# Attention over a memory in halves: queries, keys, probabilities and values as high and low parts, loaded head by head

## What is computed

```python
mem_n = rmsnorm(mem, mem_norm)                                   # 256 x 1024
mk, mv = jnp.split(mem_n @ mem_w_kv[i], 2, axis=-1)              # 4 heads of 256 columns each
...
def memory_attention(zq, mem_k, mem_v):                          # zq: part of h @ w_in, 512 x 1024
    s = jnp.einsum('bthd,bmhd->bhtm', q, mem_k) * (XA_DIM ** -0.5)
    p = jax.nn.softmax(s, axis=-1)
    o = jnp.einsum('bhtm,bmhd->bthd', p, mem_v)
```

## Time and profile before

| | us |
|---|---|
| median of three runs | 2362.25 (2361.05 to 2362.57) |
| profiled execution | 2362.44 |
| its span | 2360.7 |
| TensorE busy | 2340.6 (99%) |
| VectorE busy | 1197.9 (51%) |
| ScalarE busy | 743.0 (31%) |
| GpSimd busy | 263.3 (11%) |
| clock granted to TensorE | 0.998 |

### The profile page before, as it was taken

The page is one execution under the profiler, slowest core; times in us unless marked ns, Lnnn a source line. Parts: engine busy times, 40 slices in busy tenths (PEclk is TensorE's granted clock), DMA queues, the critical chain, the costliest instruction groups (busy, mean ns, idle before and its releaser), DMA issues.

```text
span 2360.7 us, 29488 instructions
## 1 busy us (share of the span) xinstructions
PE 2340.6 (99%) x10944; PEld 1943.6 (82%) x10944; DVE 1197.9 (51%) x1411; ACT 743.0 (31%) x1005; POOL 263.3 (11%) x235
## 2 busy tenths in 40 slices
PE   9999999999999999999999999999999999999998
PEld 9988888877888888888878888887788888888887
DVE  6654443446888654444445444344337644444422
ACT  4432222234444322222223223123333322322322
POOL 3400001111333420000110000120001212000000
PEclk9999999999999999999999999999999999999999
DMA  7733333332222333333333333333233233333322
GB/s 233 215 98 96 94 94 98 98 107 63 72 71 78 100 91 97 98 98 98 97 90 91 96 98 98 98 98 98 70 94 88 83 96 107 98 98 94 93 95 92
DMA packets 400691, 234.32 MB, mean 99 GB/s; under 512 B 7692, under 2 KB 386672, under 8 KB 400624
## 3 DMA queue, kind: packets, MB, share of 16 engines
q1 hardware_dynamic: 397328, 223.37, 32.1%
q0 software_dynamic: 3280, 10.02, 1.2%
q10 hardware_dynamic: 16, 0.00, 0.0%
HBM read 227.07 MB, written 6.29 MB: 99 GB/s over the span
## 4 chain that ended last, share of the span: by engine, by line
PE 95%; DVE 2%; ACT 1%; issue 1%; DMA 0%; POOL 0%; ACTq 0%; DVEq 0%; SPq 0%; POOLq 0%
PE acc L1012 26%; PE acc L1014 26%; PE acc L1013 26%; PE acc L766 1%; PE acc L768 1%; PE acc L767 1%; PE mix L398 1%; PE mix L385 1%; PE acc L249 1%; PE acc L251 1%; PE acc L250 1%; PE mix L250 1%; PE mix L249 1%; PE mix L251 1%; PE mix L833 1%
## 5 line engine op out<-in xcount | busy, mean ns | idle before, releaser
L1174 DVE TENSOR_TENSOR w_lo<-raw,w_hi 128x1024 fp32r<-128x1024 f32 (+1 forms) x422 | 548.3, 1302 | 658.4 <-ACT w_hi L1444 647.8
L1012 PE MATMUL acc<-h_hi,w_hi 128*128 128x512 f32 x1920 | 759.2, 395 | 7.5 <-DVE h_lo L1236 5.3
L1014 PE MATMUL acc<-h_hi,w_lo 128*128 128x512 f32 x1920 | 748.4, 390 | 0.0
L1013 PE MATMUL acc<-h_lo,w_hi 128*128 128x512 f32 x1920 | 747.9, 390 | 0.0
L1444 ACT ACTIVATE w_hi<-raw 128x1024 fp32r<-128x1024 f32 (+1 forms) x422 | 436.5, 1038 | 354.3 <-DMA raw<-in_ffn_w_out_dram 222.0
L1012 PEld LDWEIGHTS acc<-h_hi,w_hi 128*128 128x128 f32 x1920 | 361.3, 188 | 85.2 <-DVE h_lo L1236 6.6
L1013 PEld LDWEIGHTS acc<-h_lo,w_hi 128*128 128x128 f32 x1920 | 361.2, 188 | 77.0 <-issue 3.7
L1014 PEld LDWEIGHTS acc<-h_hi,w_lo 128*128 128x128 f32 x1920 | 360.9, 188 | 75.6
L1012 PE MATMUL acc<-act_hi,w_hi 128*128 128x512 f32 (+1 forms) x976 | 368.7, 378 | 2.6 <-DVE act_lo L1185 1.7
L1014 PE MATMUL acc<-act_hi,w_lo 128*128 128x512 f32 (+1 forms) x976 | 366.2, 375 | 0.0
L1013 PE MATMUL acc<-act_lo,w_hi 128*128 128x512 f32 (+1 forms) x976 | 366.1, 375 | 0.0
(11 more groups left out here) (214 smaller groups left out, 1779.0 us busy)
## 6 DMA issues: line engine op xcount, KB each, us to landing
raw<-in_ffn_w_in_dram SPq DMA_DIRECT2D x176, 512.0 KB, 3.7
raw<-in_ffn_w_out_dram SPq DMA_DIRECT2D x70, 512.0 KB, 4.0
raw<-in_hgrn_w_in_dram SPq DMA_DIRECT2D x40, 512.0 KB, 3.7
raw<-in_gmlp_w_in_dram SPq DMA_DIRECT2D x40, 512.0 KB, 3.6
raw<-in_mem_w_kv_dram SPq DMA_DIRECT2D x32, 512.0 KB, 4.2
raw<-in_gmlp_w_out_dram SPq DMA_DIRECT2D x24, 512.0 KB, 4.0
raw<-in_ffn_w_out_dram SPq DMA_DIRECT2D x24, 384.0 KB, 3.4
raw<-in_hgrn_w_out_dram SPq DMA_DIRECT2D x16, 512.0 KB, 4.0
```

What stands on the lines that cost most here:

```text
L1012: pe.matmul(bank, w_hi[:, j, i, :], hi, start=(start and i == 0), stop=False)
L1013: pe.matmul(bank, w_hi[:, j, i, :], lo, start=False, stop=False)
L1014: m = pe.matmul(bank, w_lo[:, j, i, :], hi, start=False, stop=(stop and i == last))
L1174: dve.tensor_tensor(w_lo[:, j, 0:nkb], raw[:, j, 0:nkb], f32(w_hi[:, j, 0:nkb]), ALU.subtract).then_inc(w_lo_ready, 1)
```

## The change

Keys and values are split when they are taken: for a K block VectorE's take stays, ScalarE writes the rounded half (`k_top`), VectorE the rest (`k_rest`); for a V block ScalarE takes two banks as before and then writes their rounded halves, VectorE subtracts in the next quad (`v_rest`), and after the last quad. A store carries both halves, 256 KB for 128 before, from buffers of its own (`k_parts`, `v_parts`), and waits for the rest half; the rounded half of a lane waits until the lane's last store has landed. The second copies of a V pair wait for the first ones.

In the attention q becomes a take (VectorE), a rounding copy (ScalarE) and a rest (VectorE); the turned probabilities a rounding copy (as the copy before) and a rest. The products are three fp32r matmuls each. The K and V of heads 0 and 1 are loaded when the phase begins, those of heads 2 and 3 into the same places when head 0's and 1's products are done (`load_later`, on GpSimd's queue): 8 loads of 256 KB, then 8 more.

```diff
-    k_scratch = nc.dram_tensor("k_scratch", (16, P, MEM), F32).ap()
-    v_scratch = nc.dram_tensor("v_scratch", (16, P, MEM), F32).ap()
+    k_scratch = nc.dram_tensor("k_scratch", (16, 2, P, MEM), F32).ap()
+    v_scratch = nc.dram_tensor("v_scratch", (16, 2, P, MEM), F32).ap()
...
+        k_parts = act_hi[:, 8:12, :].rearrange("p j (z m) -> p j z m", z=2)
+        v_parts = act_hi[:, 12:16, :].rearrange("p j (z m) -> p j z m", z=2)
...
+                slots = halves_at(kv_at, 8).rearrange("p (n b) (k m) -> p n b k m", n=2, k=2)
+                self.k = [[slots[:, n, part, :, :] for part in range(2)] for n in range(2)]
+                self.v = [[slots[:, n, 2 + part, :, :] for part in range(2)] for n in range(2)]
...
+                self.q_hi, self.q_lo = halves_at(q_hi_at, 4), halves_at(q_lo_at, 4)
+                self.p = work[:, p_at:p_at + 2, :].rearrange("p b (k m) -> p (b k) m", k=2)
+                self.pT_hi, self.pT_lo = halves_at(pT_hi_at, 2), halves_at(pT_lo_at, 2)
...
+                return 16 * 2 * (2 * self.layer + h // 2 + 1)
+            def load_half(self, pool, into, scratch, h, done):
+                b = DB * self.layer + 2 * h
+                for z in range(2):
+                    pool.dma_start(into[:, 2 * z:2 * z + 2, :],
+                                   scratch[b:b + 2, z].rearrange("b p m -> p b m")).then_inc(done, 16)
...
+                for h in range(2):
+                    self.load_half(pool, self.k_into[h], k_scratch, h, sem(f"k_loaded{h}"))
+                    self.load_half(pool, self.v_into[h], v_scratch, h, sem(f"v_loaded{h}"))
+            def load_later(self, pool):
+                for h in range(2, XH):
+                    pool.wait_ge(sem("scores_done"), XH * self.layer + h - 1)
+                    self.load_half(pool, self.k_into[h % 2], k_scratch, h, sem(f"k_loaded{h % 2}"))
+                    pool.wait_ge(sem("pv_done"), XH * self.layer + h - 1)
+                    self.load_half(pool, self.v_into[h % 2], v_scratch, h, sem(f"v_loaded{h % 2}"))
...
-                    pe.wait_ge(sem("pT_ready"), 2 * (n + 1))
+                    pe.wait_ge(sem("pT_lo"), 2 * (n + 1))
+                    pe.wait_ge(sem(f"v_loaded{h % 2}"), self.loads(h))
+                    v_hi, v_lo = self.v[h % 2]
                     for dv in range(2):
+                        cols = slice(dv * P, (dv + 1) * P)
                         for mb in range(MB):
-                            m = pe.matmul(mix[2 + dv][:], self.v[:, h, mb, dv * P:(dv + 1) * P], self.pT[:, mb, :],
-                                          start=(mb == 0), stop=(mb == MB - 1))
+                            pe.matmul(mix[2 + dv][:], v_hi[:, mb, cols], self.pT_hi[:, mb, :], start=(mb == 0), stop=False)
+                            pe.matmul(mix[2 + dv][:], v_hi[:, mb, cols], self.pT_lo[:, mb, :], start=False, stop=False)
+                            m = pe.matmul(mix[2 + dv][:], v_lo[:, mb, cols], self.pT_hi[:, mb, :], start=False,
+                                          stop=(mb == MB - 1))
                     m.then_inc(sem("pv_done"), 1)
...
+                    pe.wait_ge(sem(f"k_loaded{h % 2}"), self.loads(h))
+                    pe.wait_ge(sem("q_lo"), 2 * (n + 1))
                     if n:
                         pe.wait_ge(sem("exp_done"), TB * n)
+                    k_hi, k_lo = self.k[h % 2]
                     for tb in range(TB):
+                        bank, toks = mix[tb // 2][:, (tb % 2) * MEM:(tb % 2 + 1) * MEM], slice(tb * P, (tb + 1) * P)
                         for d in range(2):
-                            m = pe.matmul(mix[tb // 2][:, (tb % 2) * MEM:(tb % 2 + 1) * MEM],
-                                          self.qT[:, 2 * (h % 2) + d, tb * P:(tb + 1) * P],
-                                          self.kT[:, 2 * h + d, :], start=(d == 0), stop=(d == 1))
+                            at = 2 * (h % 2) + d
+                            pe.matmul(bank, self.q_hi[:, at, toks], k_hi[:, d, :], start=(d == 0), stop=False)
+                            pe.matmul(bank, self.q_hi[:, at, toks], k_lo[:, d, :], start=False, stop=False)
+                            m = pe.matmul(bank, self.q_lo[:, at, toks], k_hi[:, d, :], start=False, stop=(d == 1))
                     m.then_inc(sem("scores_done"), 1)
...
                     dve.wait_ge(unit_done, LANES * self.ph.q0 + u + 1)
-                    if u >= 4:
-                        dve.wait_ge(sem("scores_done"), XH * self.layer + u // 2 - 1)
-                    dve.tensor_tensor(self.qT[:, u % 4, :], acc[u % LANES][:], rstd[:], ALU.mult).then_inc(acc_read, 1)
+                    dve.tensor_tensor(tmp[:, 4 + u % 2, :], acc[u % LANES][:], rstd[:], ALU.mult).then_inc(acc_read, 1)
+                    dve.wait_ge(sem("q_hi"), n + 1)
+                    dve.tensor_tensor(self.q_lo[:, u % 4, :], tmp[:, 4 + u % 2, :], f32(self.q_hi[:, u % 4, :]),
+                                      ALU.subtract).then_inc(sem("q_lo"), 1)
+                if s % 2 == 0 and s >= 4 and (s - 4) // 2 < XH:
+                    n = XH * self.layer + (s - 4) // 2
+                    for mb in range(MB):
+                        dve.wait_ge(sem("pT_hi"), 2 * n + mb + 1)
+                        dve.tensor_tensor(self.pT_lo[:, mb, :], mix[2 + mb][:], f32(self.pT_hi[:, mb, :]),
+                                          ALU.subtract).then_inc(sem("pT_lo"), 1)
...
+                    act.wait_ge(acc_read, self.ph.g0 + u + 1)
+                    if u >= 4:
+                        act.wait_ge(sem("scores_done"), XH * self.layer + u // 2 - 1)
+                    act.activation(self.q_hi[:, u % 4, :], tmp[:, 4 + u % 2, :], ACT.Copy).then_inc(sem("q_hi"), 1)
...
-                        act.activation(self.pT[:, mb, :], mix[2 + mb][:], ACT.Copy).then_inc(sem("pT_ready"), 1)
+                        act.activation(self.pT_hi[:, mb, :], mix[2 + mb][:], ACT.Copy).then_inc(sem("pT_hi"), 1)
...
-                mixes[i] = (Attention(0, ph, 0, 24), Hgrn(ph))
+                mixes[i] = (Attention(0, ph, 0, 24, 8, 28, 30, 34), Hgrn(ph))
             if kind == "gmlp_in":
-                mixes[i] = (Attention(1, ph, 24, 32), Gmlp(ph))
+                mixes[i] = (Attention(1, ph, 24, 32, 0, 36, 38, 4), Gmlp(ph))
...
+                def k_rest(it, j):
+                    dve.wait_ge(sem("k_hi"), LANES * kv_turn_of(it) + j + 1)
+                    dve.tensor_tensor(k_parts[:, j, 1, :], tmp[:, j, 0:MEM], f32(k_parts[:, j, 0, :]),
+                                      ALU.subtract).then_inc(sem("k_lo"), 1)
+                def v_rest(it, at):
+                    dve.wait_ge(sem("v_hi"), LANES * kv_turn_of(it) + at + 1)
+                    dve.tensor_tensor(v_parts[:, at, 1, :], tmp[:, at, MEM:2 * MEM], f32(v_parts[:, at, 0, :]),
+                                      ALU.subtract).then_inc(sem("v_lo"), 1)
...
+                    if KV_QUADS[it] == "k" and j:
+                        k_rest(it, j - 1)
+                    if it and j == 0 and KV_QUADS[it - 1] == "k":
+                        k_rest(it - 1, 3)
+                    if it and KV_QUADS[it - 1] == "v" and j in (0, 2):
+                        v_rest(it - 1, j)
+                        v_rest(it - 1, j + 1)
...
+                if it == len(KV_QUADS) - 1:
+                    for at in range(LANES):
+                        v_rest(it, at)
...
-                    at = 2 * p + mb
+                    at, n = 2 * p + mb, LANES * turn + 2 * p + mb
+                    if turn:
+                        act.wait_ge(sem("v_lo"), n - LANES + 1)
+                    act.activation(tmp[:, at, MEM:2 * MEM], acc[at][:, 0:MEM], ACT.Copy,
+                                   scale=small[:, 60 + mb:61 + mb]).then_inc(sem("v_staged"), 1)
+                for mb in range(MB):
+                    at, n = 2 * p + mb, LANES * turn + 2 * p + mb
+                    act.wait_ge(sem("v_staged"), n + 1)
                     if turn:
                         act.wait_ge(sem(f"mv_stored{at}"), 16 * turn)
-                    act.activation(tmp[:, at, MEM:2 * MEM], acc[at][:, 0:MEM], ACT.Copy,
-                                   scale=small[:, 60 + mb:61 + mb]).then_inc(sem("v_staged"), 1)
+                    act.activation(v_parts[:, at, 0, :], tmp[:, at, MEM:2 * MEM], ACT.Copy).then_inc(sem("v_hi"), 1)
+            def k_top(it, j):
+                turn = kv_turn_of(it)
+                act.wait_ge(acc_read, LANES * turn + j + 1)
+                if turn:
+                    act.wait_ge(sem(f"k_stored{j}"), 16 * turn)
+                act.activation(k_parts[:, j, 0, :], tmp[:, j, 0:MEM], ACT.Copy).then_inc(sem("k_hi"), 1)
...
+                    if kind == "k" and j:
+                        k_top(it, j - 1)
+                    if it and j == 0 and KV_QUADS[it - 1] == "k":
+                        k_top(it - 1, 3)
...
-                pool.wait_ge(acc_read, n + 1)
+                pool.wait_ge(sem("k_lo"), n + 1)
```

(7 more changed lines are left out.)

26 lines of the change are left out of this document (10 added, 16 removed).

## The result

| | before | changed |
|---|---|---|
| median of nine runs, us | 2362.25 (2358.02 to 2363.83) | 2367.47 (2365.22 to 2370.78) |
| profiled execution: span, us | 2360.7 | 2363.5 |
| TensorE busy, us | 2340.6 | 2331.0 |
| VectorE, ScalarE, GpSimd busy, us | 1197.9, 743.0, 263.3 | 1233.6, 761.8, 289.6 |

The changed kernel takes 1.0026 times as long, with a 95% interval from 1.0017 to 1.0035: 6 us more, between 4 and 8, by the ratio of the runs, 5.2 by the medians. The forecast was 2367.0.

A forecast was written before the change was run, and what follows sets the result against it. TensorE was taken to bound the kernel, with 95% of the chain that ended last. The terms -10.2 + 1.9 + 9.4 + 3.5 = +4.6 on 2362.4 gave 2367.0 us, range 2358 to 2379.

The forecast's parts named there:

- The attentions, -10.2: Attention on TensorE, both layers: three half products replace each float32 product, gaining 5.1 us a layer, 10.2 in all.
- End of the attention in layer 0, +1.9: Step 10 of layer 0: VectorE subtracts before the mixer's next take, delaying the mixer's chain; cost 1.9 us, between 0 and 3.
- The quads, +9.4: Memory projections, units in fours: added copies, residuals and larger stores exceed the weight chain's slack; loss 9.4 us, bounds 4 and 16.
- The end of the projections, +3.5: Projections' end, first ffn units: later stores delay the sum of squares and fourth w_lo; loss 3.5 us, bounds 1 and 6.
- The projections absorb the additions: Rival, chance 0.15: idle stretches of VectorE and ScalarE take up much of the projections' new work; 2358.7 us.
- The loads become the bound: Rival, chance 0.27: in the projections each load beside a store lands 1.4 us later, +14 us in all; 2376.
- The half products aren't cheaper: Rival, chance 0.01: in the attentions half products cost today's record price, three for two, 27 us more; 2404.

The follow-up runs named there:

- the attention alone: Changed kernel with the memory projections of the kernel before, so K and V aren't split and their lower halves are wrong: 2354.66 us (0.9967).
- the run with narrow squares: Changed kernel with GpSimd's squares and their sum in the projections over 8 of 512 columns: 2358.79 us (0.9982); same edit to the kernel before: 2359.19 us.
- the run with the squares first: Changed kernel, but in quads 6 and 7 GpSimd's squares stand ahead of the quad's first store, not the fourth: 2367.34 us (1.0016).
- the run with the rest later: Changed kernel, but at step 10 of layer 0 VectorE takes the mixer's unit before it subtracts the turned probabilities: 2365.61 us (1.0016).
- the projections alone: Changed kernel's projections with the attention of the kernel before, reading upper halves alone: 2378.12 us (1.0061).

## Why the prediction was right, and where it was not

**The time.** 2367.0 was forecast, 2367.47 measured, +0.26% with an interval whose lower end lies at 0.17%. The terms were right too, but two of them for reasons that the runs took apart.

**The attentions, -10.2.** Right: 1.28 us at each of the three places per layer, 5.1 a layer in the table, and -7.6 for the attention alone with the 1.9 of layer 0 in it (8.3 expected). All that was costed at nothing there did cost nothing.

**End of the attention in layer 0, +1.9.** Right: 1.85 in the trace; with the order changed the median is 1.9 lower and the wait 1.5 shorter. The step on which it rested, that VectorE's queue puts the subtraction ahead of the take, is the one that the run undid.

**The quads, +9.4.** The sum was near (8.3 up to unit 31 in the trace, 1 us of it an old wait that went), its places were not. The prediction spread it over all six quads by adding each copy and rest to the chain and taking off the slack: 2.0 in quad 2, 1.2 and 1.5 in quads 3 and 4, 1.1 and 0.8 in quads 5 and 6, 1.4 in quad 7, and 1.4 for the stores. Measured were 4.0 in quad 2, nothing in quad 3, 2.0 in quad 4, 1.9 in quad 5, 1.1 in quad 6, and none in quad 7. The step that failed is the pricing of GpSimd's squares as some 2 us: the run with narrow squares left 1.5 us of the 8.3, so they are worth 6.9. What was missed is that the squares themselves move, with the stores ahead of them, under operations that ran alone before: the 8-column steps in quad 2 were not in the sum at all. The stores' size was put at 1.4 and 0.5 and is worth 3.1 in the trace.
The rule quoted from the Trainium skill ("SBUF — State Buffer", section "SBUF: two separate sides") was the part to lean on. For w_lo, for the rests of 256 columns (0.42 to 1.51 us) and for steps of 8 columns (0.32 to 1.56) the trace agrees that VectorE and GpSimd exclude each other for whole instructions (w_lo until 69.01, then the sum until 70.16, then the next w_lo until 71.24).

**The end of the projections, +3.5.** Too small: +6.2 (+7.4, less the 1.2 that the earlier w_lo gives back, which was foreseen). Of the wait before the sum of squares, 3.1 us were forecast and 4.7 measured. Its mechanism was right, store by store, and TensorE's start (4.2 us behind unit 31) too; the w_lo and the rests ahead of the third store came 1.2 us later than assumed, since a square lay on them (the w_lo at 120.22 took 2.61 us). The term that was missing is the clock: behind the wait TensorE ran at 0.51 for 5.2 us, with 0.43 us from one 512-wide matmul to the next, which takes 0.23 otherwise: half the pace for 5.2 us, some 2.5 us. That the wait for the third w_lo, 0.8 in the prediction, stood hidden behind the first one is what the run with the squares first showed.

**What cancelled.** By the two traces the quads were 1 too high and the end 2.7 too low: without the clocks at units 100 and 225 the traces are 6.1 apart, where 4.6 was the sum, and the medians 5.2. How much too high the quads were isn't firm. The same projections had unit 31 done 9.2 us behind the kernel before in the run with the rest later and 11.4 in the one with the projections alone, and 8.3 is the figure of the fastest execution. A hit within half a us is partly luck; the range, 2358 to 2379, is the better measure of what was known.

**The rivals.** *The projections absorb the additions*: no, 14.5 us by unit 35. *The loads become the bound*: not by 14 us. From quad 2 on three loads landed after the 5.5 us that the prediction named, at 5.5 to 5.8, all in quad 6, and ScalarE's wait ahead of unit 24 ended with a store's landing; the doubled stores are worth 3.1 us in the trace. *The half products aren't cheaper*: no.

## What to carry to other kernels

Look first for the stage in which an engine already waits before work is put where the data are produced: here splitting the keys and values, with the doubled stores that go with it, cost 14.5 us in the projections and nothing in the attention. When GpSimd's list mixes waits with arithmetic, a longer wait moves the arithmetic, and what it moves under on VectorE has to be looked up row by row. Before a wait is costed as the loss, look at what else becomes ready during it: where two waits lie over each other, as these two did, taking one out gives nothing.

## What the runs showed of the hardware

A VectorE step over 8 columns (0.16 us alone, 0.32 with the end of a sum beside it) takes 1.56 beside a square of 1.05 on GpSimd, and ends with the square: a small VectorE operation isn't spared. GpSimd is held the other way round as well: its sum of 1.3 us takes 2.16 beside a w_lo.

GpSimd's store issues are another matter. Beside issues alone, over the first 140 us of all fourteen traces, none of 94 w_lo took more than 1.23 us and none of 20 rests of 256 columns more than 0.43. The block of h takes 0.48 us alone; of 59 beside issues 42 took no longer, and 17 did, all at two places (0.52 to 0.70 near 31 us, 1.07 to 1.12 near 86 us). The second place in the changed kernel:

```profile
86.00 1.12 DVE L1280 TENSOR_SCALAR tmp<-x,vecs 128x512 f32<-128x512 f32 x1
...
86.15 2.17 POOL L1755 DMA_DIRECT2D k_scratch<-act_hi  x3
```

Why these and not the others stays open.

Behind a wait of 4.7 us TensorE's clock was at 1.2 GHz (0.51), and behind one of 3.6 us in another kernel (0.50). Behind waits of 2.1 to 2.2 us it fell in some traces and stayed in others, at the same two places, with 1.5 us at stake each time. At one of them, unit 225, this went with no difference between the kernels that I can name.
